# Block 1's value projections: column tiles of 512 in place of 256, weight rows in the outer loop and the two token blocks inside it, computed in two parts of four row blocks

## The reference, cut to what matters

```python
proj = (h @ w_in).astype(jnp.float32)              # h: 256 tokens x 1024
(cu, cb, cc, rq, rk, rv, rg, gq, gk, gv, gr, ga_down,
 gate_a, gate_b, gate_c) = split_columns(proj)     # rv, gv: 512 columns each
...
s = jnp.einsum('bhid,bhjd->bhij', qi, ki) * decay_mask      # retention, per chunk
intra = jnp.einsum('bhij,bhjv->bhiv', s, vi)                # vi: from rv
...
intra = jnp.einsum('bhij,bhjv->bhiv', s, vi)                # gated attention, vi: from gv
```

## Time and profile before

| | before |
|---|---|
| median of 3 runs | 2707.72 us (2706.95 to 2708.73) |
| the profiled execution | 2704.53 us, of which the span in the profile is 2702.7 us |
| PE matmuls | 2639.3 us busy, 98% of the span, 16130 instructions |
| DVE, ACT, POOL busy | 1357.6, 1282.3, 1620.4 us |
| values of block 1, first layer | from 63.40 us to 98.94 us of the span, where step `("c", 0)` begins |
| values of block 1, second layer | from 570.46 us to 606.59 us |

### The profile page before, as it was taken

How to read it: one execution, slowest core, us unless ns; L and a number is a source line. 1 busy time by engine, 2 the same in 40 slices (tenths; PEclk the granted TensorE clock), 3 DMA queues, 4 the chain that set the end, 5 groups by cost and what they waited for, 6 DMA issues and landing times.

```text
span 2702.7 us, 41596 instructions
## 1 busy us (share of the span) xinstructions
PE 2639.3 (98%) x16130; PEld 2262.8 (84%) x16130; DVE 1357.6 (50%) x2441; ACT 1282.3 (47%) x2042; POOL 1620.4 (60%) x1252
## 2 busy tenths in 40 slices
PE   8999999999999999999999999999999999999999
PEld 8998888889887888786788888888888888999888
DVE  5885533277654345875532334431333855335644
ACT  6464544455544454446333433442443564445654
POOL 6778688778786885432333344444444635458787
PEclk9999999999999999999999999999999999999999
DMA  6458676534777653211112223223232423234455
GB/s 215 141 183 285 225 257 218 165 132 160 261 264 245 236 175 116 87 63 55 63 65 84 71 86 101 79 95 101 93 102 85 135 86 109 94 110 156 164 187 164
DMA packets 145012, 386.13 MB, mean 143 GB/s; under 512 B 11968, under 2 KB 64448, under 8 KB 144832
## 3 DMA queue, kind: packets, MB, share of 16 engines
q1 hardware_dynamic: 144832, 383.61, 42.6%
HBM read 382.51 MB, written 1.05 MB: 142 GB/s over the span
## 4 chain that ended last, share of the span: by engine, by line
POOL 52%; issue 46%; PE 1%; POOLq 1%; DMA 0%; DVE 0%; ACT 0%; DVEq 0%
POOL w_lo L956 52%; PE bank L1014 1%; POOLq L953 0%; PE bank L1018 0%; DMA raw<-stream 0%; POOLq L960 0%; PE bank L1000 0%; PE bank L999 0%; PE bank L998 0%; POOLq L956 0%; ACT fc L1934 0%; DVE fc L2630 0%; DVE xs L2359 0%; DVE bank L2642 0%; DVE hid L2645 0%
## 5 line engine op out<-in xcount | busy, mean ns | idle before, releaser
L956 POOL TENSOR_TENSOR w_lo<-raw,w_hi 128x512 fp32r<-128x512 f32 x1248 | 1620.2, 1328 | 1073.8 <-ACT w_hi L1512 1071.8
L1512 ACT ACTIVATE w_hi<-raw 128x1024 fp32r<-128x1024 f32 x624 | 656.0, 1054 | 384.4 <-DMA raw<-stream 158.9
L998 PE MATMUL bank<-hl,w_hi 128*128 128x256 f32 (+1 forms) x2000 | 683.3, 342 | 2.4 <-POOL w_lo L956 1.0
L999 PE MATMUL bank<-hl,w_hi 128*128 128x256 f32 (+1 forms) x2000 | 668.9, 334 | 0.0
L1000 PE MATMUL bank<-hl,w_lo 128*128 128x256 f32 (+1 forms) x2000 | 668.8, 334 | 0.0
L998 PEld LDWEIGHTS bank<-hl,w_hi 128*128 128x128 f32 x2000 | 380.1, 190 | 46.3 <-issue 6.5
L999 PEld LDWEIGHTS bank<-hl,w_hi 128*128 128x128 f32 x2000 | 380.2, 190 | 40.6 <-issue 3.6
L1000 PEld LDWEIGHTS bank<-hl,w_lo 128*128 128x128 f32 x2000 | 380.0, 190 | 37.8
L1014 PE MATMUL bank<-hl,w_hi 128*128 128x512 f32 x1296 | 339.9, 395 | 3.4 <-POOL w_lo L956 3.1
L1014 PEld LDWEIGHTS bank<-hl,w_hi 128*128 128x128 f32 x1296 | 231.9, 189 | 51.5 <-issue 9.9
L1018 PEld LDWEIGHTS bank<-hl,w_lo 128*128 128x128 f32 x1296 | 179.0, 190 | 13.0
(11 more groups left out here) (331 smaller groups left out, 4072.4 us busy)
## 6 DMA issues: line engine op xcount, KB each, us to landing
raw<-stream SPq DMA_DIRECT2D x624, 512.0 KB, 3.3
spare_lo<-stream SPq DMA_DIRECT2D x32, 512.0 KB, 6.0
mix<-stream SPq DMA_DIRECT2D x32, 512.0 KB, 6.4
spare_hi<-stream SPq DMA_DIRECT2D x32, 512.0 KB, 5.8
xs<-x_rows SPq DMA_DIRECT2D x4, 256.0 KB, 4.0
xs<-ctx_rows SPq DMA_DIRECT2D x1, 1024.0 KB, 13.3
out_rows<-xs SPq DMA_DIRECT2D x8, 128.0 KB, 3.4
dec<-decay SPq DMA_DIRECT2D x1, 768.0 KB, 10.5
```

What stands on the lines that cost most here:

```text
L956: last = nc.gpsimd.tensor_tensor(w_lo[:, unit % SPLIT, part], raw[:, unit % RAW, part], w_hi[:, unit % SPLIT, part], ALU.subtract)
L998: nc.tensor.matmul(acc, wh, x[:, 0, k, c0:c1], start=k == 0, stop=False)
L999: nc.tensor.matmul(acc, wh, x[:, 1, k, c0:c1], start=False, stop=False)
L1512: nc.scalar.activation(w_hi[:, n % SPLIT, :], raw[:, n % RAW, :], ACT.Copy).then_inc(hi_ready, 1)
```

## The change

The tiles of `rv` and `gv` become one tile of 512 columns each, four units, in each layer. `wide_values` computes such a tile in two calls, one at each of the two old places in `MIX1`: the first call takes row blocks 0 to 3, the second 4 to 7. A row block is read once, for both blocks of 128 tokens, which accumulate in two banks that stay in use from the first call to the end of the second. A matmul covers 512 columns in place of 256, and there are half as many. A unit is released by `unit_used` as soon as its two row blocks are done. `take_wide_values` has no copy out of a bank in the first part; it has two splits there (units first+4 and first+5 of the tile), and in the second part one split and then both copies, of 512 columns.

```diff
-        for v in range(2):
-            put("rv", "w_in", l, span(rv + 256 * v, 256))
-        for v in range(2):
-            put("gv", "w_in", l, span(gv + 256 * v, 256))
+        put("rv", "w_in", l, span(rv, 512))
+        put("gv", "w_in", l, span(gv, 512))
...
-            if t.wide == 2:
+            if t.wide > 1:
                 n = 2 if t.array == "w_in" else T2 // P
...
+            def wide_values(first, half):
+
+                t, n, b = TILES[at["tile"]], PLACE.first_out[at["tile"]], PLACE.first_block[at["tile"]]
+                accs = [bank_of(n + i) for i in range(2)]
+                for k in range(half * t.k // 2, (half + 1) * t.k // 2):
+                    u, j = (b + 4 * k) // UNIT, (b + 4 * k) % UNIT
+                    wait_unit(u)
+                    wh, wl = w_hi[:, u % SPLIT, j * P:(j + 4) * P], w_lo[:, u % SPLIT, j * P:(j + 4) * P]
+                    for i, acc in enumerate(accs):
+                        c = first + i * P
+                        nc.tensor.matmul(acc[:, :], h_hi[:, k, c:c + P], wh, start=k == 0, stop=False)
+                        nc.tensor.matmul(acc[:, :], h_hi[:, k, c:c + P], wl, start=False, stop=False)
+                        last = nc.tensor.matmul(acc[:, :], h_lo[:, k, c:c + P], wh, start=False, stop=k == t.k - 1)
+                        if k == t.k - 1:
+                            last.then_inc(tile_done, 1)
+                    if k < t.k - 1 and (b + 4 * (k + 1)) % UNIT == 0:
+                        last.then_inc(unit_used, 1)
+                at["tile"] += half
...
-                        values(c0)
+                        wide_values(c0, i)
...
+            def take_wide_values(dst, half):
+
+                first = PLACE.first_block[at["tile"]] // UNIT
+                if half == 0:
+                    split_through(first + 1 + SPLIT)
+                    at["freed"] = first + 1
+                    return
+                n = next_tile()
+                for i in range(2):
+                    E.need(tile_done)
+                    nc.scalar.activation(dst[:, i, :], banks[PLACE.bank[n + i]][:, :], ACT.Copy).then_inc(tile_out, 1)
```

More of the change, by code:

```diff
@@ L1663, in _ @@
                     elif step == "rv":
-                        take_values(rv, i)
+                        take_wide_values(rv, i)
                     elif step == "gv":
-                        take_values(gv, i)
+                        take_wide_values(gv, i)
                     elif step == "c":
@@ L2165, in _ @@
                     if step in ("g", "r", "rv", "gv", "c", "rg", "gr"):
-                        n = {"g": 5, "r": 2, "rv": 2, "gv": 2, "c": 3, "rg": RH, "gr": GH}[step]
+                        n = {"g": 5, "r": 2, "rv": 2 * i, "gv": 2 * i, "c": 3, "rg": RH, "gr": GH}[step]
                         outs[step] = outs[step, i] = E.later(tile_out, n)
```

## The result

The changed kernel took 2711.57 us (median of 20 runs, 2706.77 to 2717.25), the kernel before 2706.93 us (20 runs beside them, 2703.05 to 2710.41). The ratio is 1.002, with a 95% interval from 1.0014 to 1.0026: the change costs 4 to 7 us. The profiled execution took 2710.72 us, its span 2708.9.

The account below looks back on a forecast made before the run. PE was taken as the bound, with DVE close behind. Savings of 2.4 and 1.4 us, taken back by a wait at the first mix, summed to 0.0 within 0.3 us: 2707.5 us against the median, range 2704.6 to 2709.9 (8 in 10).

Parts of the forecast that it names:

- the second rival: Waits at score 1 and first mix lower PE's clock: 2.4 us a layer, 2709.9 us for one, 2712.3 for both; 11%.
- a delay at the first mix: First mix at 82.3 to 82.6 us (was 80.61) and 589.9 to 590.1 (was 588.93), taking back the matmuls' gain; 55%.
- the matmuls and the waits for POOL: In the value steps: wide matmuls save 2.4 us in all, shorter waits of PE for POOL save 1.4 us.
- the 3.8: Full saving in us of matmuls and waits for POOL together in the value steps, if nothing else moves.
- The third rival: In the value steps, a wide matmul is no cheaper than two narrow ones: 1.2 us lost in both layers, 2708.7 us; 5%.
- the first mix and what follows it: `k_dec` and diff 3 slow under POOL, `rv` copies and first mix late, then PE regains ground up to step c.
- 16.56 us: Predicted time from first mix to step c: three mixes, two value parts, two takes and scores; 18.33 us before.
- Step c: End of the value stretch: forecast to move by -0.1 to +0.2 us in the first layer, -0.1 to +0.1 in the second.
- the clock at 11%: The second rival's chance: a clock drop behind the first mix, decided where the single wait comes near 2.9 us.
- the 1.7 us taken: Predicted cost of each clock drop behind the first mix; a wait long enough for it costs some 0.7 more.
- Further on a gain or loss passes through unchanged: Behind step c DVE follows PE, no later step sees another order, and any gain or loss stays as it is.

Follow-up runs that it names:

- narrow_parts: The changed kernel with each 512-column value matmul made two of 256 columns again, in halves of the same bank: 2709.57 us, ratio 1.0012 to before.
- lagged_splits: The changed kernel, wide matmuls and copies kept, with ACT's splits within `rv` back at their old places: 2706.04 us, ratio 0.9999 to before.
- busy_at_mix: The changed kernel with four unread products of constants in PE's wait ahead of each first mix: 2708.94 us, ratio 1.0008 to before.
- pinned_banks: The changed kernel with the first bank of `gv` chosen so that the other 600 tiles keep before's banks: 2709.61 us, ratio 1.002 to before.
- before_busy: The kernel before with dummy products in two later waits of PE, five near 699 us and four near 992 us: 2706.61 us, ratio 1.0005 to before.
- before_again: A second profile of the kernel before, unchanged, one execution: 2703.99 us.

## Why the prediction was wrong

Forecast were 2707.5 us, with a range to 2709.9; measured 2711.57. The nearest case was the second rival, slower by the clock, in both layers.

The forecast was for a change too small to tell, and its cause, a delay at the first mix that takes back the saving, is there. Three steps of it failed.

**Right: the matmuls and the waits for POOL.** The distance is 0.2276 us (0.2275 taken), and narrow_parts puts the saving at 0.53 us for two steps (0.6). No wait for POOL is left in the value steps. lagged_splits shows both gains where nothing takes them back: 1.1 + 1.4 = 2.5 us of the 3.8. The third rival, a wide matmul that is no cheaper, is out.

**Right in mechanism, short in size: the first mix and what follows it.** `k_dec` was to cost 1.1 us more and costs 1.07. But POOL's second unit followed the first at once, so the addition `L2224` (1.69 us) also fell under POOL, and I had allowed 0.4 for that; diff 3 itself was free again (0.69). Counted from the first value matmul, the mix was to come at 18.9 to 19.2 us and came at 19.44; in the second layer at 19.4 to 19.6 and came at 19.64. From mix to c I had 16.56 us and it takes 16.8: 0.25 us of the small pauses between the steps, which I had seen in before, stay, and my sum had no term for them. Step c was to move by -0.1 to +0.2 and -0.1 to +0.1; with the clock up it moves by +0.7 and +0.3. The sum is so 1.0 us too low at the end of the two stretches, the first of the three steps that failed, though for the first layer that loss does not arrive at the second (below).

**Wrong: the clock at 11%.** I let this rival decide where a single wait comes near 2.9 us, and the forecast itself had no term for the clock. The waits were 1.8 us at the mix, behind 0.2 to 1.0 us at score 1 (2.0 and 2.8 us together in the change, where I had 2.3 and 2.9), and that is enough at times: 5 of 10 first mixes with this delay and no dummies have a drop behind them, 0 of 4 with dummies, and none of 14 that come at 17.2 to 18.5 us. A drop cost 1.5 to 1.6 us (38.01 - 36.45, 37.87 - 36.25), a long one 2.8 to 2.9 (39.20 - 36.45, 39.33 - 36.45); the 1.7 us taken were right for the short kind. The five sum to 10.3 us over five profiles: about 2.1 us for each execution. That is a small sample: were the dummies without effect, 0 of 4 would still come about once in eight times. The earlier trace rows had shown me a long wait with a drop and a short one without, one execution of each; I drew the line at the long one. The short one, near 190 us, has a drop in three of the 14 profiles.

**Wrong: "Further on a gain or loss passes through unchanged".** The loss of the first layer does not pass through: PE waits for ACT near 190 us in any case, and there 0.7 us become -0.1 and +0.5. And at two places behind the values it matters when a load lands, and whether DVE's instructions fall under POOL. Near 992 us the wait was 2.3 us in the profiles of all kernels with wide matmuls where no dummies fill it, with a drop behind it in six of seven; before had 1.35 and 0 and no drop. This is worth 2.4 to 2.5 us against the first profile of before (0.9 where no drop follows) and up to 3.9 against the second. The wait near 702 us costs some 1.5 us more where a drop follows it (+0.8 and -0.6 in the two profiles of the change). The wait near 992 us does not come from the order of the steps: narrow_parts has that order and no wait there. It goes with the length of the program, by a load that lands late in before and narrow_parts, beside a transfer of instructions, and not in the wide kernels; that is read from the traces and not tested. The shift of the banks was tested and is out.

**The account in place of mine.** From the first value matmul on, the two profiles of the change take some 6.7 us more than those of before: nothing in the first layer, 2.5 us in the second value stretch (0.3 fixed, the rest a drop), 0.3 near 699 us, 3.1 near 992 and 0.8 behind. The medians differ by 4.6 us, with an interval of 4 to 7, so the profiles overstate the loss. Both profiles of before caught short executions (2704.53 and 2703.99 us, at mean clocks of 0.997 and 0.998, where the mean over all executions of before is 0.9962 to 0.9969, by chip): before too has further drops, in executions that no profile shows. Terms read from single profiles can therefore not be added up to the 4.6 us. Only the delay of the first mix is shown by an experiment that removes it alone, lagged_splits. For the drops behind it busy_at_mix speaks, with 4 cases; for the later places there are profiles only. The clocks of all executions fit a share of the drops without saying where they fall: over 229 of them, compared within each kernel and chip, 0.001 of mean granted clock goes with 2.1 us of span (least squares), and on one chip the change with pinned banks has 0.9956 and before 0.9969, which is 2.7 of the 5.8 us between their mean spans. How the 4.6 us divide between the first mixes and the later places stays open.

## What to carry to other kernels

Ask of a faster stage which instructions it brings together: here one split moved ahead of a wait gave POOL work in a gap that DVE had used, and the chain DVE, ACT, PE took the gain of the stretches back and more; moving it back keeps 2.5 us of saving in the stretches, though no median here is faster beyond its interval. A wait of TensorE, where it is the bounding engine, costs its length and, in some executions, a clock drop of 1.6 us or more, so a forecast needs a chance for it at every wait that grows. Of 4 us that an analysis finds in a 2707 us kernel, as much can be lost or won at places that the change never touches: a wait further on can swallow a loss, and a program of another length loads its instructions at other moments. So profile each kernel more than once, lay the profiles beside each other at the same matmuls, and put their spread into the range.

## What the hardware showed that I had not expected

- A DVE instruction of 8 to 24 columns takes 0.17 us or less alone and up to 1.3 us beside POOL's subtraction (`half_w`, 0.17 and 1.32), as much longer as one of 512 columns (0.68 and 1.75). The price is by instruction, not by column. Not every one pays it: of the six above, the first at L2042 and the last at L2043 take 0.17 and 0.16 us, each right behind one that has paid. The Trainium skill, SBUF — State Buffer, section SBUF: two separate sides, says that the port pair that DVE and GpSimd share is locked for a whole instruction and the loser blocks, on DVE's side for instructions in a two-port mode or with two inputs in SBUF; no run shows in which mode the small ones run. The rows agree for the small instructions that pay: what they lose, 1.1 to 1.2 us, is about one POOL instruction (11.38 us for nine, 1.26 each).
- The granted clock fell behind a wait of PE of 1.8 us with 1.0 or even 0.2 us more ahead of it, in 5 of 10 cases, and for two different lengths. One stretch so takes up to 2.9 us more or less (36.45 and 39.33 us, in the second layer of busy_at_mix and pinned_banks; 38.01 and 39.20 in two profiles of the same program).
- With four dummy products (1.9 us) in the wait ahead of the first mix the clock stayed up in 4 of 4 cases, and the mix was not delayed; where no wait was, the same four cost 1.5 us (before_busy and before_again near 992 us).
- A transfer of 16 KB of instructions that begins 0.5 to 2 us behind the request for a unit of 512 KB goes with a load of 4.6 us in place of 3.3 (medians of 27 and 597 loads in the change's profile).
